# Expert bodies of TensorE in another order, row counts in registers, and narrower constant products

## The chip, the cores and the metric

The kernel runs on one core of a Trainium2 chip. The metric is the device time of one execution in microseconds, median of three runs. TensorE (PE) multiplies matrices and loads its weights beside that (PEld), VectorE (DVE) and ScalarE (ACT) work on vectors, GpSimd (POOL) does odd jobs, SyncE (SP) issues most transfers. Each engine has an instruction stream of its own and waits on counters in shared semaphores.

## The reference

Two layers of a hybrid encoder over 256 tokens of width 1024. Each layer is a token mixer (differential attention, mLSTM, latent attention) and a channel mixer: a dense SwiGLU in layer 0, eight experts in layer 1, of which every token takes its two best.

```python
def swiglu(u, wg, wu, wd):
    return (jax.nn.silu(u @ wg) * (u @ wu)) @ wd

def reference(...):
    for l in range(DEPTH):                      # 2
        shift, scale, gate = ada_modulation(c, w_ada[l, 0], b_ada[l, 0])
        h = rmsnorm(x, g_norm[l, 0]) * (1.0 + scale) + shift
        x = x + gate * rmsnorm(hybrid_mixer(h, positions, l, ...), g_norm[l, 1])
        shift, scale, gate = ada_modulation(c, w_ada[l, 1], b_ada[l, 1])
        h = rmsnorm(x, g_norm[l, 2]) * (1.0 + scale) + shift
        if l % 2 == 0:
            y = swiglu(h, w_gate_d[l // 2], w_up_d[l // 2], w_down_d[l // 2])
        else:
            y = moe_swiglu(h, w_router[l // 2], b_router[l // 2], w_gate_e[l // 2], w_up_e[l // 2], w_down_e[l // 2])
        x = x + gate * rmsnorm(y, g_norm[l, 3])
    return x
```

In `moe_swiglu` the router's two best experts of each token are found, the tokens are sorted by expert, `swiglu` is applied to each expert's rows with its own weights (1024 x 3584 twice, 3584 x 1024 once), and each token's two results are added with their gates.

## The kernel before

Layer 0 and the mixer of layer 1 take the first 680 us. Their weights come through a ring of seven slots. What this case is about is the loop over the eight experts, from about 680 us to the end, and how each engine finds its code in it.

**Rows.** The number of rows of each expert is known only on the chip (tensor `cnt`, filled by the router). It is rounded up to one of six sizes (`NVAR`, 32, 64, 128, 160, 192, 256), and for each size there is a body of code. With these inputs the experts 0 to 7 take the bodies 32, 32, 128, 64, 160, 32, 192 and 64. In the trace a body is known by its line: 32 and 64 rows by L1449 (gate and up) and L1463 (down), in `expert_whole`; 160 and 192 by L1492 and L1507, in `expert_wide`; 128 by L1584 and L1623, in `expert_split`. The last two kinds take part of the weights as pairs of narrower numbers that ScalarE and VectorE make (`parts`), the first kind takes them as they are.

**Stages.** The 3584 columns of an expert are 14 stages. In each PE multiplies the rows (`mixT`, in the code `xe`) by the gate and up weights into the bank `PG`, ScalarE takes Silu, VectorE the product, PE turns it (`turn`, L1435), VectorE copies it out (L2581), and PE multiplies it by the down weights into `Y`. The first stage of the wide bodies uses the banks `TRB` too.

**Weights.** An expert's weights are 42 pieces of 1 MB ("uses"), in 14 slots (`ring` and `arena`). SP issues one transfer for each (`expert_use`, L787) in the order of use, when PE has signalled its last read of the piece that was in the slot 14 uses before. So SP can be up to 14 pieces ahead of PE, and across the border between two experts too.

**Rows of the next expert.** GpSimd copies them into `xe` (L2782 for the first, L2789 in its loop) after the last gate and up product of the expert before, and raises `xe_ready`, on which PE waits ahead of each body.

**The loop.** `experts` (L670) writes the same skeleton of blocks for PE, VectorE and ScalarE: `next` counts `turn` up and ends the loop, `pick` loads this expert's count from `cnt` into the register `rows`, a chain of tests (`tree` and `not_...`, L693 and L695) compares it with the sizes, and the bodies follow, each ending in a branch to `next`, with a hint to the hardware placed at the body's head (L698). The body of 128 rows stands first, right behind the tests, and is reached by falling through all of them; the others stand behind it by size (32, 64, 160, 192, 256) and are reached by a taken branch. The tests for smaller sizes come first (L693), then those for larger ones, from 256 down (L695).

**Constant products.** `busy` (L845) lets PE multiply a constant by the identity into a bank that nobody reads. It stands in `stats` (L861), three products of 256 columns ahead of a wait for VectorE's `diag` (L880), at seven places that run one after the other through the program, and once ahead of `gather` (L1393), four products of 256 columns.

**Reading the instruction rows.** One product of 4-byte floats is carried out in several passes, and each pass is an instruction of its own in the trace: a count of x64 at L1449 is 64 passes.

## Time and profile before

| | |
|---|---|
| median of three runs | 1666.01 us (1665.38, 1666.01, 1673.49) |
| profiled execution | 1666.87 us |
| its span, first to last instruction | 1665.0 us |
| PE busy | 1475.6 us, 89% of the span |
| PEld | 1186.7 us, 71% |
| VectorE | 781.7 us, 47% |
| ScalarE | 589.5 us, 35% |
| GpSimd | 69.4 us, 4% |
| moved by DMA | 488.89 MB, mean 294 GB/s |

PE is busy for 89% of the span. That is a mean over stages with different limits: in the experts of 32 rows PE is idle for part of each stage while the DMA engines are always occupied, in the wider ones it is the other way round. Branches, register and semaphore instructions aren't counted as busy. "Issue" as the reason for idle time means that the engine waited for nothing that the profile can name: no semaphore, no transfer, no engine.

### The profile page before, as it was taken

To read this page: it belongs to the slowest core of one execution; us is meant where nothing else is said; L and a number is where in the kernel's file an instruction comes from. 1 tells how busy PE (TensorE), PEld (TensorE's weight loads), DVE (VectorE), ACT (ScalarE), POOL (GpSimd) and SP (SyncE) were. 2 spreads that over 40 slices of the span, in tenths; PEclk is the share of its full clock that TensorE was granted. 3 is DMA by queue.
4 is the path that set the end of the run, shared out by engine and by line. 5 is a ranking of instruction groups with operands and counts; after the bars stand their busy time and mean duration, and the time that the engine had idled before them with its cause. 6 is when DMAs were issued, how large, how long until landed. Compare 5 with 4: busy or idle time off the path is not lost.

```text
span 1665.0 us, 30777 instructions
## 1 busy us (share of the span) xinstructions
PE 1475.6 (89%) x12430; PEld 1186.7 (71%) x12431; DVE 781.7 (47%) x1097; ACT 589.5 (35%) x793; POOL 69.4 (4%) x67
## 2 busy tenths in 40 slices
PE   5999899999999998765679999999997589999894
PEld 3868778999977886644447875589885468888452
DVE  2574565666546654200019861166761046665112
ACT  2445244444343532100017750055641035554101
POOL 0010100000010111000000000000000000000002
PEclk9999999999999999987779999999999889999997
DMA  9645367745423627899999999997778996666893
GB/s 349 234 154 201 157 250 284 296 177 203 163 96 127 228 77 317 367 425 424 424 425 426 426 421 421 425 425 287 263 250 361 424 424 265 224 226 225 308 426 140
DMA packets 69183, 488.89 MB, mean 294 GB/s; under 512 B 7744, under 2 KB 7776, under 8 KB 11168
## 3 DMA queue, kind: packets, MB, share of 16 engines
q1 hardware_dynamic: 66800, 479.94, 72.3%
q10 hardware_dynamic: 1648, 4.59, 0.8%
q8 instruction: 117, 1.92, 0.5%
q0 software_dynamic: 576, 2.10, 0.4%
q14 instruction: 42, 0.34, 0.1%
HBM read 482.66 MB, written 3.93 MB: 292 GB/s over the span
## 4 chain that ended last, share of the span: by engine, by line
PE 45%; DMA 10%; issue 4%; DVE 2%; SPq 1%; ACT 1%; POOL 0%; ACTq 0%; POOLq 0%; DVEq 0%
PE PG L1449 9%; DMA arena<-in_experts 6%; PE PG L1507 4%; PE PG L1571 4%; PE Y L1534 4%; PE Y L1463 4%; PE TRB L1507 4%; DMA ring<-in_experts 3%; PE TRB L1513 3%; PE PG L1513 3%; PE Y L1623 2%; PE Y L1525 2%; PE TRB L1435 2%; SPq L787 1%; PE PG L1492 1%
## 5 line engine op out<-in xcount | busy, mean ns | idle before, releaser
L2581 DVE COPY arena<-TRB 128x64 f32<-128x64 f32 (+1 forms) x70 | 17.6, 252 | 339.9 <-PE TRB L1435 339.9
L1449 PE MATMUL PG<-ring,mixT 128*32 128x128 f32 (+1 forms) x1920 | 119.8, 352 | 56.9 <-issue 56.7
L1687 ACT ACTIVATE rope<-PG 64x128 f32<-64x128 f32 (+2 forms) x84 | 27.1, 323 | 373.8 <-PE PG L1449 352.1
L1449 PEld LDWEIGHTS PG<-ring,mixT 128*32 128x32 f32 (+1 forms) x1920 | 91.6, 139 | 88.1 <-issue 73.0
L951 PE MATMUL PG<-h_parts,parts 128*128 128x512 f32 x432 | 152.9, 394 | 1.4 <-DVE arena L2459 1.4
L1687 ACT ACTIVATE parts<-ring 128x2048 fp32r<-128x2048 f32 x81 | 151.8, 1901 | 6.1 <-DMA ring<-in_weights 2.8
L1449 PE MATMUL PG<-arena,mixT 128*32 128x128 f32 (+1 forms) x1664 | 99.5, 343 | 47.6 <-issue 47.6
L1449 PEld LDWEIGHTS PG<-arena,mixT 128*32 128x32 f32 (+1 forms) x1664 | 76.7, 135 | 75.4 <-issue 62.2
L953 PE MATMUL PG<-h_parts,parts 128*128 128x256 f32 x432 | 121.8, 282 | 0.0
L2444 DVE TENSOR_TENSOR parts<-ring,parts 128x2048 fp32r<-128x2048 f32 x42 | 95.1, 2290 | 29.2 <-ACT parts L1687 29.2
L2565 DVE TENSOR_TENSOR parts<-arena,parts 128x2048 fp32r<-128x2048 f32 x42 | 95.3, 2288 | 17.0 <-PE Y L1525 14.4
L2565 DVE TENSOR_TENSOR ring_parts<-ring,parts 128x2048 fp32r<-128x2048 f32 x39 | 88.4, 2288 | 25.0 <-PE Y L1525 13.2
L951 PEld LDWEIGHTS PG<-h_parts,parts 128*128 128x128 f32 x432 | 81.2, 188 | 19.8 <-DVE arena L2459 1.6
L953 PEld LDWEIGHTS PG<-h_parts,parts 128*128 128x128 f32 x432 | 81.3, 188 | 0.0
L1687 ACT ACTIVATE parts<-arena 128x2048 fp32r<-128x2048 f32 x42 | 78.9, 1902 | 4.7 <-PE PG L1571 4.1
L918 PE MATMUL Y<-parts 128*128 128x256 f32 x224 | 63.5, 283 | 0.2 <-DVE parts L2468 0.2
L920 PE MATMUL Y<-parts 128*128 128x256 f32 x224 | 63.4, 283 | 0.0
L919 PE MATMUL Y<-parts 128*128 128x256 f32 x224 | 63.4, 283 | 0.0
L2134 DVE TENSOR_TENSOR ring_parts<-ring,ring_parts 128x2048 fp32r<-128x2048 f32 (+1 forms) x24 | 52.8, 2199 | 18.9 <-ACT ring_parts L1687 18.8
L2565 DVE TENSOR_TENSOR parts<-arena,scr_parts 128x2048 fp32r<-128x2048 f32 x21 | 48.1, 2293 | 26.6 <-ACT scr_parts L1687 26.6
L1687 ACT ACTIVATE ring_parts<-ring 128x2048 fp32r<-128x2048 f32 (+1 forms) x24 | 43.8, 1837 | 41.3 <-PE Y L1258 30.2
L1687 ACT ACTIVATE arena<-PG 128x512 f32<-128x512 f32 x29 | 17.3, 597 | 114.5 <-PE PG L953 105.6
(385 smaller groups left out, 2881.4 us busy)
## 6 DMA issues: line engine op xcount, KB each, us to landing
ring<-in_experts SPq DMA_DIRECT2D x168, 1024.0 KB, 16.7
arena<-in_experts SPq DMA_DIRECT2D x168, 1024.0 KB, 17.5
ring<-in_weights SPq DMA_DIRECT2D x116, 1024.0 KB, 6.4
ring<-in_weights SPq DMA_DIRECT2D x4, 512.0 KB, 4.9
ypairs<-hT ACTq DMA_DIRECT2D x3, 512.0 KB, 5.7
tok<-in_x SPq DMA_DIRECT2D x1, 1024.0 KB, 9.2
result<-scr SPq DMA_DIRECT2D x2, 512.0 KB, 2.6
ring<-in_weights SPq DMA_DIRECT2D x2, 432.0 KB, 5.5
```

Source lines behind the costliest of these rows:

```text
L918: mm(out_, w_hi[w][:, c], x[0], start=first, stop=False, skip_group_check=True)
L951: mm(PG[:, m, :].rearrange("p (i t) -> p i t", i=2), w_hi[d % SPLITS][:, c], h_parts[:, :, k, :], start=(k == 0), stop=False, skip_group_c ...
L953: last = mm(PG[:, m, 0:T], w_lo[d % SPLITS][:, c], h_hi[:, k, :], start=False, stop=(k == KD - 1), skip_group_check=True)
L1449: last = mm(bank[i * n:(i + 1) * n, 0:width], xe[:, k, 0:n], w[k // 4][:, k % 4, i * width:(i + 1) * width], start=(k == 0), stop=(k == KD ...
L1463: last = mm(o, actT[:, s % 2, f, 0:n], w[:, f, c:c + width], start=(s == 0 and f == 0), stop=(s == STAGES - 1 and f == 1))
L1507: last = mm(both, hi[:, k, i // 2, i % 2, :], h_parts[:, :, h * KD // 2 + k, 0:n], start=(h == 0 and k == 0), stop=False, skip_group_check ...
L1513: last = mm(bank[:, 0:n], lo[:, k, i // 2, i % 2, :], h_parts[:, 0, h * KD // 2 + k, 0:n], start=False, stop=(h == 1 and k == KD // 2 - 1) ...
L1534: last = mm(o, a[:, s % 2, f, :], w[:, f, c:c + width], start=(opens and s == 0 and f == 0), stop=(closes and s == STAGES - 1 and f == 1))
L1571: last = mm(bank, x[j][:, h * KD // 2 + k, :], w[:, k, :], start=(opens and k == 0), stop=(closes and k == KD // 2 - 1))
L1687: return nc.scalar.activation(out_, in_, func, **kw)
L2444: V.tensor_tensor(w_lo[d % SPLITS], ring[:, slot_of[slot_of_dense(d)], :, :].rearrange("p k c -> p (k c)"), w_hi[d % SPLITS].bitcast(F32), ...
L2565: V.tensor_tensor(w_lo_e[q % SLOTS_E], ring_e[q % SLOTS_E].rearrange("p k c -> p (k c)"), w_hi_e[q % HI].bitcast(F32), ALU.subtract).then_ ...
```

## The change

1. `experts` takes the order of the bodies as a table, `layout`; its first entry is the body behind the tests. PE gets (32, 192, 64, 160, 128, 256). VectorE and ScalarE keep the default, which is the order of before.
2. On each of the three engines the eight counts are loaded ahead of the loop into eight registers (`to_come`). The tests read the first of them, and `next` moves all the others down by one. The block `pick` is gone.
3. `busy` cuts its products: six of 128 columns for three of 256 in `stats`, sixteen of 64 for four of 256 ahead of `gather`.

```diff
--- before.py
+++ after.py
@@ -667,23 +667,26 @@
             u, n = proj_use(l, key)
             return (ring_parts[:, slot_of[i], 0:n].rearrange("p (k c) -> p k c", k=KD) for i in (u + 1, u))
 
-        def experts(eng, name, emit, first_variant=128):
+        def experts(eng, name, emit, layout=(128, 32, 64, 160, 192, 256)):
+
+            first_variant = layout[0]
 
             def label(x):
                 return f"{name}_{x}"
 
             own = [eng.engine]
             turn = eng.alloc_register(label("e"))
-            rows = eng.alloc_register(label("rows"))
+            to_come = [eng.alloc_register(label(f"rows_{i}")) for i in range(NE)]
+            rows = to_come[0]
+            for i in range(NE):
+                eng.reg_load(to_come[i], cnt[0:1, i:i + 1])
             eng.reg_mov(turn, 0)
-            eng.br(label("pick"))
+            eng.br(label("tree"))
             with nc.body(label("next"), valid_engines=own):
                 eng.reg_add(turn, turn, 1)
-                eng.br_lt(turn, NE, on_true=label("pick"), on_false=label("done"))
-            with nc.body(label("pick"), valid_engines=own):
-                e = eng.snap(turn, min_val=0, max_val=NE - 1)
-                eng.reg_load(rows, cnt[0:1, bass.ds(e, 1)])
-                eng.br(label("tree"))
+                for i in range(NE - 1):
+                    eng.reg_mov(to_come[i], to_come[i + 1])
+                eng.br_lt(turn, NE, on_true=label("tree"), on_false=label("done"))
 
             tests = [n for n in NVAR if n < first_variant] + [n for n in reversed(NVAR) if n > first_variant]
             after = [label(f"not_{n}") for n in tests[:-1]] + [label(first_variant)]
@@ -693,7 +696,7 @@
                         eng.br_lt(rows, n + 1, on_true=label(n), on_false=then)
                     else:
                         eng.br_lt(rows, NVAR[NVAR.index(n) - 1] + 1, on_true=then, on_false=label(n))
-            for n in sorted(NVAR, key=lambda n: n != first_variant):
+            for n in layout:
                 with nc.body(label(n), valid_engines=own):
                     back = eng.mark_branch_hint_location()
                     emit(eng.snap(turn, min_val=0, max_val=NE - 1), n)
@@ -874,7 +877,7 @@
                     last = mm(bank[:, b:b + 1], s4[:, b * P:(b + 1) * P], ones[:, 0:1], start=True, stop=True)
                 last.then_inc(tr_full, 1)
                 bank = take_tr((kind, n, "laid"))
-                busy(bank, 3)
+                busy(bank, 3, 2)
                 pe.wait_ge(diag_ready, q + 1)
                 for b in range(TB):
                     last = mm(bank[:, b * P:(b + 1) * P], ones[:, :], diag[:, b, :], start=True, stop=True)
@@ -1387,7 +1390,7 @@
                skip_group_check=True).then_inc(tr_full, 1)
 
 
-            busy(xg_banks[0], 4)
+            busy(xg_banks[0], 4, 4)
 
             def gather(k, b, part, columns, first=False):
                 return mm(xg_banks[k][:, columns], part[:, b, k * P:(k + 1) * P], sel[:, b, columns],
@@ -1663,7 +1666,7 @@
                 pe.wait_ge(xe_ready, e + 1)
                 (expert_whole if n < P else expert_split if n % P == 0 else expert_wide)(e, n)
 
-            experts(pe, "pe", expert)
+            experts(pe, "pe", expert, layout=(32, 192, 64, 160, 128, 256))
 
             for b in range(TB):
                 for k in range(KD):
```

**PE at the loop's head.** The rows below are the instructions in the order of the program. Before, from the last products ahead of the loop (L1393) through counting (L681), the end test (L682), the load of the count (L685) and the tests to the body of 128 rows (from L1421):

```order
L1393 MATMUL TRB<-parts,h_parts 128x512 x8
L679 UNCONDITIONAL_BRANCH
L681 REGISTER_ALU
L682 COMPARE_AND_BRANCH
L684 ISA
L685 TENSOR_LOAD cnt
L686 UNCONDITIONAL_BRANCH
L693 COMPARE_AND_BRANCH x2
L695 COMPARE_AND_BRANCH x3
L698 BRANCH_PREFETCH_HINT
L699 ISA
```

After, the same place:

```order
L1396 MATMUL TRB<-parts,h_parts 128x512 x8
L682 TENSOR_LOAD cnt x8
L684 UNCONDITIONAL_BRANCH
L686 ISA
L689 COMPARE_AND_BRANCH
L698 COMPARE_AND_BRANCH x5
L701 BRANCH_PREFETCH_HINT
L702 ISA
L1424 ISA
L1452 MATMUL PG<-ring,mixT 32x128 x64
```

The loads of the counts stand ahead of the loop, five tests of one kind lead to the body behind them, and that body begins with products of 32 rows.

**PE where one body ends and the next stands.** Before, the end of the body of 128 rows (L1623) and the head of that of 32 rows (L1449):

```order
L1623 MATMUL Y<-parts 128x512 x4
L1623 MATMUL Y<-parts,arow_parts 128x512 x4
L1623 MATMUL Y<-parts 128x512 x4
L700 UNCONDITIONAL_BRANCH
L698 BRANCH_PREFETCH_HINT
L699 ISA
L1421 ISA
L1449 MATMUL PG<-ring,mixT 32x128 x64
```

After, the end of the body of 32 rows (L1466) and the head of that of 192 rows (L1495):

```order
L1461 REGISTER_ALU
L1466 MATMUL Y<-arena 32x256 x8
L703 UNCONDITIONAL_BRANCH
L701 BRANCH_PREFETCH_HINT
L702 ISA
L1424 ISA
L1495 MATMUL PG<-mixT,ring 128x192 x8
```

What stood between the bodies of 128 and 64 rows (32) now stands ahead of all, followed by 192; likewise 64 follows 192, 160 follows 64, and 128, which was first, follows 160.

## Rows read from the trace of the kernel before

**Rows 1.** Busy time by stage: us, busy of each engine, PEclk, DMA share, GB/s

```profile
690.00:1078.00 388.00, 317.80 (x3254) 227.02 (x3253) 126.90 (x157) 101.62 (x117) 8.11 (x4) 0.91 1.01 424
...
1142.00:1254.00 112.00, 110.49 (x833) 98.07 (x833) 76.82 (x63) 61.10 (x62) 1.90 (x1) 1.00 0.71 259
```

**Rows 2.** PE in time: start, length, line, operation, passes, [idle before <-what ended it]

```profile
664.03 1.06 PE L849 MATMUL TRB<-con 128*128 128x128 f32 x8
...
665.56 1.97 PE L849 MATMUL PG<-con 128*128 128x256 f32 x8
...
669.22 0.95 PE L1393 MATMUL PG<-parts,h_parts 128*128 128x256 f32 x6 [1.69 <-DVE parts L2535]
...
681.01 4.28 PE L1449 MATMUL PG<-ring,mixT 128*32 128x128 f32 x76 [4.04 <-issue]
...
765.89 3.22 PE L1449 MATMUL PG<-ring,mixT 128*32 128x128 f32 x56 [7.38 <-issue]
...
771.33 3.70 PE L1449 MATMUL PG<-ring,mixT 128*32 128x128 f32 x72 [2.22 <-issue]
...
866.98 7.13 PE L1584 MATMUL PG<-ring,mixT 128*128 128x512 f32 x16 [0.74 <-issue]
...
881.30 1.21 PE L1623 MATMUL Y<-parts 128*128 128x512 f32 x4 [1.35 <-DVE arow_parts L2573]
...
990.91 3.24 PE L1449 MATMUL PG<-ring,mixT 128*64 128x256 f32 x28
...
995.02 4.11 PE L1449 MATMUL PG<-ring,mixT 128*64 128x256 f32 x36 [0.86 <-issue]
...
1067.83 3.67 PE L1449 MATMUL PG<-arena,mixT 128*64 128x256 f32 x32 [1.12 <-issue]
...
1082.92 1.62 PE L1492 MATMUL TRB<-mixT,ring 128*128 128x160 f32 x10 [1.50 <-issue]
...
1259.16 3.22 PE L1449 MATMUL PG<-ring,mixT 128*32 128x128 f32 x56 [4.59 <-issue]
...
1344.30 4.65 PE L1492 MATMUL PG<-mixT,ring 128*128 128x192 f32 x16 [6.91 <-issue]
...
1551.99 9.17 PE L1449 MATMUL PG<-ring,mixT 128*64 128x256 f32 x64 [5.66 <-issue]
```

**Rows 3.** Branches of PE's sequencer by switch: ns min/median/max, first and last start in us

```profile
L693 PEldq COMPARE_BRANCH  x1: 6561/6561/6561, 673.9 to 673.9; - x1
...
L693 PEldq COMPARE_BRANCH  x1: 6488/6488/6488, 758.9 to 758.9; - x1
...
L695 PEldq COMPARE_BRANCH  x3: 65/65/68, 866.3 to 866.6; - x3
...
L693 PEldq COMPARE_BRANCH  x2: 67/210/352, 988.9 to 989.1; - x2
...
L695 PEldq COMPARE_BRANCH  x3: 65/68/447, 1076.6 to 1076.9; - x3
...
L693 PEldq COMPARE_BRANCH  x1: 4007/4007/4007, 1254.6 to 1254.6; - x1
...
L695 PEldq COMPARE_BRANCH  x2: 68/3179/6290, 1337.5 to 1337.6; - x2
...
L693 PEldq COMPARE_BRANCH  x2: 67/2520/4972, 1546.4 to 1546.5; - x2
```

**Rows 4.** The page, DMA queues: packets, MB, share of 16 engines

```profile
q8 instruction: 117, 1.92, 0.5%
```

**Rows 5.** GpSimd in time: the first expert's rows, two copies

```profile
677.10 2.02 POOL L2782 COPY mixT<-arena 128x1536 f32<-128x1536 f32 x2 [21.36 <-PE TRB L1393]
```

**Rows 6.** Line 685, the count's load: ns min/median/max, first and last start

```profile
L685 PEldq TENSOR_LOAD <-cnt x8: 302/306/495, 673.4 to 1546.0; - x8
```

**Rows 7.** ScalarE's sequencer at the head of its last body, window 1550 to 1557

```profile
L698 ACTq BRANCH_PREFETCH_HINT  x1: 55/55/55, 1555.5 to 1555.5; - x1
```

**Rows 8.** Line 880: idle time before it by releaser, us and times

```profile
  DVE diag L2086: 4.2, 8
```

## The prediction

> **What bounds the kernel now.** I read the page first, then the busy time by stage, then PE's instructions in order of time around each change of expert, then the branches of PE's sequencer, which the page's busy times leave out. From 690 to 1078 us the DMA engines are occupied all the time (share 1.01); from 1142 to 1254 they are at 0.71 while PE is at 110.49 of 112 us [rows 1]. So experts 0, 1 and 5 (32 rows) run at the pace of their weights, experts 2, 4, 6 and 7 (128, 160, 192, 64 rows) at PE's, and expert 3 (64 rows) starts at PE's pace and is caught by its weights at its end: two stages there begin only when their weights have landed, after 1.03 us (at 1060.54, not shown) and 1.12 us [rows 2]. From this follows what a gap of PE between two experts costs: nothing between experts 0 and 1, and all of it ahead of a body at PE's pace. Ahead of a body that waits for weights it costs the time by which the first freed slot comes later.
>
> Such gaps there are: 4.04, 7.38, 0.74, 4.59, 6.91 and 5.66 us ahead of bodies, and 2.22, 0.86, 1.50 us inside them, all "issue" [rows 2]. Under them lie branches. PE's branches take 0.06 to 0.09 us when they fall through, but 6.56, 6.49, 4.01, 6.29 and 4.97 us when they jump to the body of experts 0, 1, 5, 6 and 7; the jumps to the bodies of experts 3 and 4 took 0.35 and 0.45 us, and expert 2 was reached by falling through [rows 3]. PE's code arrives by DMA: 117 packets of 16 KB [rows 4], which is 256 instructions of 64 bytes. The rule that I take from these rows: a jump is cheap when its target stands in the packet with which the body that ran before ended (64 after 32, 160 after 64), or in the packet of the loop's tests, which every body brings back at its end; a body that has not been read lately costs a fetch. Where the packet ends soon after the target, a second wait follows: 56 products after the start of the 32-row body PE stands still for 2.22 us [rows 2].
>
> **The new order, body by body.** The experts' rows are 32, 32, 128, 64, 160, 32, 192, 64. In front of the tests now stands 32 instead of 128; 192 follows 32, 64 follows 192, 160 follows 64. Counting the built program's instructions from the places of the second waits, the packets end 96 instructions after the start of the 32-row body, 39 after 192, 143 after 64, 128 after 160, and 8 after 128.
>
> *Expert 0.* The 6.56 us branch becomes a fall-through, but PE can't begin before GpSimd's copy of the rows is done at 679.1 [rows 5]. PE begins at 679.2 instead of 681.01, the first slot is freed as much earlier, and all transfers behind it shift: -2.0. Eight register loads ahead of it, 0.3 us each [rows 6], begin while PE still works on its queue (673.4) and end before 679.
>
> *Expert 1.* 7.38 us saved under saturated DMA: 0.
>
> *Expert 2* was the fall-through and is now far off. Nearest rows: the jump ahead of expert 1, made under the same full DMA: 7.38 idle, then from 765.89 to 771.33 until the second packet is there. With only 8 instructions in the first packet nearly nothing runs in between, so both count: 7.38 + 5.44 - 0.74 as it is now = 12.1. After such a stall PE runs at 1.2 GHz for a while: 64 products took 9.17 us at 1551.99 where 32 took 3.67 at 1067.83 [rows 2], so 1.8 us more. Against it, a wait of 1.35 us for VectorE in the first stage goes, since the helpers get ahead. Together +12.5; at least 0 (body found at hand), 7.1 with one fetch, at most 15.
>
> *Expert 3.* The 0.35 us jump becomes a fetch of 4.0 to 6.5, taken as 5.5. The sequencer jumps at 989.1, 1.8 us before the array has finished at 990.9 [rows 2, 3]: 5.5 - 1.8 + 0.4 to the first product = 4.1 idle, + 1.8 for the clock, - 0.86 (143 instructions last through the next fetch): +5.0; from 0 to 8. PE, now some 15 us late, no longer meets the two waits for weights at this expert's end: -2.15. Transfers are issued by freed slots, but they are queued far ahead and move less than PE.
>
> *Expert 4.* The stall of 1.50 goes, but VectorE's own first steps bind right behind: -0.4, from 0 to -1.5.
>
> *Expert 5.* 4.59 idle becomes about 1.2 (branches and tests), and PE stays at 2.4 GHz. The first freed slot comes 5 us earlier; the transfers close up to what was queued: -4.4, from -3 to -5.
>
> *Expert 6.* 6.91 idle becomes 0.9, but after 39 instructions (17 products) a wait of about 2.9 follows (5.6 us for the fetch, as from 765.5 to 771.3, less 2.8 of work). With the clock's 1.8 back, and half of it lost again in that wait: -6.0 + 2.9 - 1.8 + 0.2 = -4.7; from -3 to -7.
>
> *Expert 7.* 5.66 idle becomes about 1.2, and the clock stays up: PE alone would gain 6.3. But ScalarE, whose code has its old order, reaches its 64-row body only at 1555.5 [rows 7]; table load, Silu and VectorE's product end near 1558, and PE's turning of them, now at 1561.1, can't be earlier: -3.0, less 0.5 for an idle PE before it: -2.5, from -1 to -6.
>
> **Tests and registers.** A load of 0.3 us [rows 6] a turn goes for eight moves of registers, and the 32-row body now takes five tests of 0.07 each instead of one. Within 0.3 us a turn either way, for the most part in the shadow of PE's queue: 0.
>
> **Narrower constant products.** Eight passes of 256 columns took 1.97 us, eight of 128 took 1.06 [rows 2]: 12 for 6 cost 0.1 us at each of seven places, where PE then waits for VectorE's diagonal, 4.2 us in eight waits [rows 8], 0.5 each. The other place has 1.69 us of waiting behind it. Cost 0; without that cover 0.8.
>
> **Sum:** -2.0 + 12.5 + 5.0 - 2.15 - 0.4 - 4.4 - 4.7 - 2.5 = +1.35 us on the profiled execution's 1666.87: 1668.2. The median of the three runs is 0.86 lower, so 1667.4.
>
> The Trainium skill ("Runtime: NRT & Kernel Launch", Instruction fetch mechanics) gives PE's instruction memory as a FIFO of 128 KiB in blocks of 256 instructions. The trace agrees: the start of the 64-row body outlived the 128-row body, but not a 32-row body and more. The same section says that there are only two lines, and a taken branch outside this window must fetch. By that rule the jump ahead of expert 3 would have cost a fetch before, too, and the change would lose nothing there; the sum would be about -3.7. The 0.35 us of that jump speaks against it.
>
> **Rivals.** (1) *One fetch ahead of expert 2*, should the packet behind the target be asked for with it: 12.5 becomes 7.1, 1662.0. Against it: three starts of the 32-row body after a fetch, two of them with a second wait. (2) *No new fetches*, should a hint at the loop's head or a larger memory hold the far bodies: the sum is -2.0 - 0.4 - 4.4 - 4.7 - 2.5 = -14.0, 1652.0. For it: two cheap jumps far back in time; against it: their targets had been read, as ends of the body before, and those of 128 and 64 would not have been. (3) *Slower: the neighbours are not kept.* A body's last packet is also where the loop's packet is called back; should the start of 192 or 64 be gone by the time of the jump, experts 6 and 7 save nothing (+7.2), and expert 2 may reach its upper price (+2.5): 1677. It decides from the point at which the target's packet has to be read again. Rows of 0.35 and 0.45 us speak against it. (4) *Nothing changes*, since all bodies wait for weights: 1666.
>
> **Chances.** Forecast 0.55 (1661 to 1673), rival 1 0.12, rival 2 0.15, rival 3 0.12, rival 4 0.06. About 0.5%, 8.3 us, is what a measurement of this kernel can tell from none: faster 0.22 (rival 2 and the low edge of rival 1), same 0.63, slower 0.15. The range goes from 1654 to 1677.
>
> **What the profile after would show.** Ahead of the first product of 128 rows an idle time near 12 us in two pieces; ahead of expert 3's first product 4; no branch over 1 us ahead of experts 0, 1, 4, 5, 6, 7; a short stall after some 17 products of 192 columns; ScalarE's table load of expert 7 still near 1556 by the old clock of events, with PE waiting for it. A single short gap ahead of expert 2 means rival 1, none rival 2; a branch of 4 us or more ahead of expert 6 or 7 means rival 3. I am wrong in the sum if delays in experts 2 and 3 turn out to be covered by transfers, or if the granted clock after the stalls is other than before.

## The result: slower by 0.47%, just outside the range

The changed kernel takes 1677.19 us (median of 18 runs, 1670.29 to 1686.4), the kernel before 1670.77 us in the same 18 rounds (1664.25 to 1680.0). The ratio on record is 1.0047, 95% interval 1.0033 to 1.0062 (the two medians by themselves give 1.0038): slower by 0.47%, 7.8 us on 1666.01. The forecast was 1667.4, a rise of 1.4 us, with a range to 1677.0. The time is 0.2 us above that range; 7.8 us on 1666.01 would be 1673.8 and inside it, since the kernel before was slower in these rounds too. Either way the rise is more than five times the one forecast. The profiled execution took 1676.06 us.

The page of the changed kernel, span, busy times and the two queues that carry code:

```profile
span 1674.3 us, 30896 instructions
PE 1484.9 (89%) x12496; PEld 1194.3 (71%) x12496; DVE 781.8 (47%) x1096; ACT 589.4 (35%) x793; POOL 69.4 (4%) x67
...
q8 instruction: 113, 1.85, 0.5%
...
q14 instruction: 42, 0.34, 0.1%
```

PE is busy for 9.3 us more, though the products are the same but for their widths. About 1.5 us of it is the narrower products (an estimate from the pages of runs 1 and 5 below, 1480.4 and 1478.9 us); for the rest, passes behind a stall run at 1.2 GHz and take longer. q8 carries PE's code, 16 KB a packet. q14 carries packets of 8 KB; several of them move when VectorE and ScalarE change bodies (six from 1548 to 1560 us in the kernel before), which is why it is read here as the queue of their code. The page of before had this second queue too; the prediction hadn't used it.

PE in order of time around the changes of expert (columns as in [rows 2]):

```profile
680.04 1.29 PE L1452 MATMUL PG<-ring,mixT 128*32 128x128 f32 x20 [2.39 <-POOL mixT L2785]
...
870.29 2.07 PE L1587 MATMUL PG<-ring,mixT 128*128 128x512 f32 x2 [7.68 <-issue]
875.38 6.93 PE L1587 MATMUL PG<-ring,mixT 128*128 128x512 f32 x9 [3.02 <-issue]
...
1004.29 3.98 PE L1452 MATMUL PG<-ring,mixT 128*64 128x256 f32 x20 [4.20 <-issue]
...
1265.91 4.19 PE L1452 MATMUL PG<-ring,mixT 128*32 128x128 f32 x128 [0.76 <-issue]
1276.83 0.76 PE L1438 MATMUL TRB<-con,rope 64*128 64x128 f32 x2 [6.74 <-DVE rope L2562]
...
1348.88 2.86 PE L1495 MATMUL PG<-mixT,ring 128*128 128x192 f32 x16 [0.45 <-issue]
1354.95 3.28 PE L1495 MATMUL TRB<-mixT,ring 128*128 128x192 f32 x12 [3.21 <-issue]
...
1555.33 7.13 PE L1452 MATMUL PG<-ring,mixT 128*64 128x256 f32 x64 [1.17 <-issue]
1567.28 0.97 PE L1438 MATMUL TRB<-con,rope 64*128 64x128 f32 x3 [4.83 <-DVE rope L2562]
```

Almost every row is where the prediction put it: expert 0 begins when GpSimd's copy is done; 7.68 and 3.02 us in two pieces ahead of expert 2, with two passes between them; 4.20 ahead of expert 3; none ahead of 5, 6 and 7; 3.21 after 16 products of 192 columns. What it had not put there are the two rows that end with "<-DVE rope": in experts 5 and 7 PE starts at once, runs through two units of gate and up products and then stands still for 6.74 and 4.83 us.

From such rows comes the account by expert. An expert ends with its last product into `Y`; the table shows how much later each kernel got there than the kernel before, from one expert's end to the next, in the profiled executions. "Ahead" is the work up to the loop, which varies from one execution to another with no reason in the loop (up to 9.5 us), "loop" is from there to the last instruction, without "ahead".

| us against before | ahead | e0, e1 | e2 | e3 | e4 | e5 | e6 | e7 | tail | loop | ratio of the times |
|---|---|---|---|---|---|---|---|---|---|---|---|
| forecast | | -2.0 | +12.5 | +2.85 | -0.4 | -4.4 | -4.7 | -2.5 | 0 | +1.35 | 1.001 |
| changed kernel | +0.7 | -4.3 | +12.8 | +2.2 | -0.7 | +0.5 | -3.2 | 0.0 | +1.4 | +8.6 | 1.0047 |
| run 1, old order | +0.4 | +1.0 | +4.9 | -3.2 | -0.7 | -1.3 | +5.3 | -0.4 | -0.3 | +5.3 | 1.0036 |
| run 2, order alone | +5.9 | -2.9 | +9.0 | +5.7 | +3.9 | -0.1 | +0.7 | +2.9 | +0.6 | +19.8 | 1.0088 |
| run 3, order on all | +2.0 | -4.3 | +13.1 | +2.4 | -0.4 | +0.8 | -3.3 | -6.2 | +0.8 | +2.8 | 1.0012 |
| run 4, 128 last | +0.2 | -3.5 | +6.6 | +2.8 | +0.7 | +0.4 | -2.7 | +0.8 | +1.4 | +6.5 | 1.0039 |
| run 5, shift alone | +2.3 | -2.8 | +5.4 | -2.6 | -0.3 | +0.2 | +4.1 | -0.3 | -0.3 | +3.3 | 1.0022 |
| run 6, 64 first, all | +1.0 | +3.8 | +0.4 | +0.1 | -1.0 | -2.2 | +1.4 | -6.8 | +0.4 | -3.9 | 0.9960 |
| run 7, 192 first, all | +3.4 | +1.0 | +1.8 | +3.9 | -0.5 | -1.8 | -3.0 | -1.4 | +1.5 | +1.5 | 0.9987 |
| run 8, 192 first, PE | +0.3 | +0.5 | +2.4 | +3.5 | -0.7 | +1.9 | -8.2 | -2.5 | +1.2 | -2.0 | 0.9982 |
| run 9, shift undone | -0.6 | +3.3 | -0.1 | 0.0 | +0.2 | +0.6 | +1.5 | -1.6 | +0.4 | +4.2 | 1.0020 |
| run 10, both mended | +8.4 | -2.2 | +7.8 | +1.4 | -0.4 | -1.0 | -2.1 | -6.5 | +0.6 | -2.3 | 0.9981 |
| run 11, 32, 128 first | +9.5 | -2.5 | +1.5 | +0.3 | +4.4 | -2.5 | +1.3 | +1.0 | -0.1 | +3.3 | 0.9988 |
| run 12, hint | +0.5 | +0.6 | +1.2 | +0.1 | +0.6 | -1.5 | -0.2 | -6.7 | -0.2 | -6.1 | 0.9959 |
| run 13, helpers alone | -3.4 | -0.2 | +0.4 | -0.5 | +0.1 | 0.0 | 0.0 | +0.2 | 0.0 | 0.0 | 1.0008 |
| run 14, no registers | +6.4 | -2.4 | +0.7 | +0.8 | +0.8 | -2.8 | +1.8 | -6.5 | +0.2 | -7.4 | 0.9963 |

One execution is not a median. Run 13 shows how little may move where PE's code stays as it was; experts 0 and 1 show how much, -2.8 us in run 5 and -0.2 in run 13, with PE's loads and order as before in both. A column of one run is taken here as good to about 2 us, that of experts 0 and 1 to 3 or 4.

### The profile page after: what moved, and what is told of

It is laid out like the page before. It is cut to its first block, busy times and chain, and to the rows that moved or that the text cites. A ratio compares the mean times of both kernels' runs of the same rounds, so it can differ in the third digit from the quotient of the medians.

```text
span 1674.3 us, 30896 instructions
## 1 busy us (share of the span) xinstructions
PE 1484.9 (89%) x12496; PEld 1194.3 (71%) x12496; DVE 781.8 (47%) x1096; ACT 589.4 (35%) x793; POOL 69.4 (4%) x67
## 3 DMA queue, kind: packets, MB, share of 16 engines
q10 hardware_dynamic: 1648, 4.59, 0.8%
## 4 chain that ended last, share of the span: by engine, by line
PE 45%; DMA 8%; issue 5%; DVE 2%; ACT 1%; SPq 1%; POOL 0%; ACTq 0%; DVEq 0%; POOLq 0%
PE PG L1452 9%; DMA arena<-in_experts 5%; PE Y L1466 4%; PE PG L1510 4%; PE Y L1537 4%; PE TRB L1510 4%; PE PG L1574 4%; DMA ring<-in_experts 3%; PE TRB L1516 3%; PE PG L1516 3%; PE Y L1626 2%; PE Y L1528 2%; PE TRB L1438 2%; SPq L790 1%; PE Y L1261 1%
## 5 line engine op out<-in xcount | busy, mean ns | idle before, releaser
L954 PEld LDWEIGHTS PG<-h_parts,parts 128*128 128x128 f32 x432 | 81.2, 188 | 19.8 <-DVE arena L2462 1.6
```

The lines of the kernel that those rows point to most:

```text
L954: mm(PG[:, m, :].rearrange("p (i t) -> p i t", i=2), w_hi[d % SPLITS][:, c], h_parts[:, :, k, :], start=(k == 0), stop=False, skip_group_c ...
```

## Experiments on the changed kernel's loss

The theory after the first look: the order costs what was forecast at expert 2, and the gains at experts 5 and 7 are hidden, since VectorE and ScalarE must fetch their own bodies there. The rivals: registers or products, and weights that come late.

**Run 1: registers and products with the old order.**

```diff
-            experts(pe, "pe", expert, layout=(32, 192, 64, 160, 128, 256))
+            experts(pe, "pe", expert)
```

> The changed kernel with the old order of bodies on TensorE: registers and narrower constant products alone. Theory (instruction packets): expert 2 is again reached by falling through (idle under 1 us), experts 5, 6 and 7 again have idle times of 4 to 7 us ahead of their first product. Only the places of the bodies in their packets move: the 192-row body now has 47 instructions left in its first packet instead of 183, so a second wait of 2 to 3 us follows within the first 25 products of expert 6; the waits of 0.86 and 1.50 us in experts 3 and 4 go. Sum +0.5 to +1 us, ratio to the kernel before 1.000 to 1.001. Rival (the register loads and moves, or the narrower products, cost the time): ratio 1.003 or more, with the loss ahead of the loop or spread over all eight switches.

Measured: ratio 1.0036 (1.0019 to 1.0053), which the theory as written excluded. The loss isn't spread, though: it sits behind the 32-row bodies, in a place that the prediction hadn't counted. The branch from the end of PE's bodies back to the loop's head, first over all eight, then those behind experts 1 and 5:

```profile
L703 PEldq COMPARE_BRANCH  x8: 201/372/5479, 760.2 to 1640.7; - x8
...
L703 PEldq COMPARE_BRANCH  x1: 4126/4126/4126, 866.8 to 866.8; - x1
...
L703 PEldq COMPARE_BRANCH  x1: 5479/5479/5479, 1337.2 to 1337.2; - x1
```

In the kernel before the same branch (L700) took 0.42 us at most. The loop's packet has to be read again too. Behind expert 5 the traces show when: in the kernel before, one packet of PE's code moves between 1326 and 1336.1 us (at 1333.3), ahead of the branch back; in run 1 none moves between 1329.5 and 1337.2, where the branch is met, and the next one comes at 1340.2. The reading that fits both is that the packet is asked for when PE enters the body's last packet. Registers and products put 136 instructions ahead of the bodies (132 of them the products, four for each product more), and with that the 32-row body ends some 75 instructions into its last packet, not 194: too few to last through a fetch. Idle ahead of expert 6 became 11.89 us, two fetches in a row:

```profile
1350.38 1.97 PE L1495 MATMUL PG<-mixT,ring 128*128 128x192 f32 x5 [11.89 <-issue]
```

The second wait that was expected within the first 25 products of expert 6 did not come: the 64 passes of 192 columns that follow run without idle time, the first 16 of them in 4.97 us instead of the 2.86 at full clock.

**Run 2: the order alone, on the kernel before.**

```diff
-        def experts(eng, name, emit, first_variant=128):
+        def experts(eng, name, emit, layout=(128, 32, 64, 160, 192, 256)):
+            first_variant = layout[0]
-            for n in sorted(NVAR, key=lambda n: n != first_variant):
+            for n in layout:
-            experts(pe, "pe", expert)
+            experts(pe, "pe", expert, layout=(32, 192, 64, 160, 128, 256))
```

> The kernel before with nothing but the new order of TensorE's bodies. Theory: the loss comes with the order, but its size depends on where each body starts in its packet. Here the 128-row body has 144 instructions left instead of 8, so expert 2 has one wait of 7 to 8 us and no second one of 3 us: its cost falls from 12.8 us to about 7. The 160-row body now has 8 left: a second wait of 2 to 5 us a few products into expert 4. The 64-row body has 23 left: 1 to 5 us more in expert 3, hidden at expert 7. Experts 5 and 7: TensorE starts 4 us earlier and waits for VectorE and ScalarE, no gain. Sum about +5 to +9 us, ratio 1.003 to 1.005. Rival (registers or products are the cause): ratio 1.000 or below.

Measured: 1.0088 (1.0061 to 1.0114), twice what was expected. Right: one wait ahead of expert 2 (8.47 us) and none behind it; 3.85 us two passes into the 160-row body, of which 8 instructions stand in its first packet:

```profile
1095.90 0.54 PE L1494 MATMUL PG<-mixT,ring 128*128 128x160 f32 x2
1100.29 2.92 PE L1494 MATMUL PG<-mixT,ring 128*128 128x160 f32 x14 [3.85 <-issue]
```

Wrong: again the ends of bodies. The 32-row body ends 82 instructions into its last packet here, and the way back takes up to 5.85 us, so that expert 6 begins after 6.80 us of idle time although its code stands next to expert 5's. So the products aren't harmless: by the count of instructions they are what put the changed kernel's bodies in better places than the order alone would (its 32-row body ends 217 instructions into a packet, and no way back there takes over 0.93 us).

**Run 5: nothing but a shift, on the kernel before.** A block of products that is never executed, between the code ahead of the loop and the loop:

```diff
-            eng.br(label("pick"))
+            if name == "pe":
+                eng.br_lt(turn, NE, on_true=label("pick"), on_false=label("pad"))
+                with nc.body(label("pad"), valid_engines=own):
+                    for _ in range(34):
+                        nc.tensor.matmul(tr[0][:, 0:8], ident, con[:, C_IOTA:C_IOTA + 8], start=True, stop=True)
+                    eng.br(label("next"))
+            else:
+                eng.br(label("pick"))
```

> The kernel before, with a block of TensorE instructions that is never executed between the code ahead of the loop and the loop: nothing is done otherwise, but all bodies stand 137 instructions later, as in the first experiment (registers and products with the old order). Theory (only the place of the code in its packets of 256 instructions cost time there): the 32-row body ends 76 instructions into its last packet instead of 194, too short to hide the fetch of the loop's packet, so TensorE's branch back to the loop takes 4 to 5.5 us after experts 0, 1 and 5; the 192-row body has 46 instructions left in its first packet. Idle time ahead of expert 2 above 4 us instead of 0.74, ahead of expert 6 near 12 instead of 6.91; ratio 1.003 to 1.004. Rival (the registers or the narrower products cost it): the idle times stay as in the kernel before, ratio 1.000.

Measured: 1.0022 (1.0003 to 1.0041), and run 1's pattern in the places where it was expected: +5.4 and +4.1 us at experts 2 and 6, with 4.83 and 10.96 us idle.

```profile
L707 PEldq COMPARE_BRANCH  x1: 3886/3886/3886, 864.9 to 864.9; - x1
...
L707 PEldq COMPARE_BRANCH  x1: 4399/4399/4399, 1338.2 to 1338.2; - x1
```

```profile
1350.40 1.96 PE L1499 MATMUL PG<-mixT,ring 128*128 128x192 f32 x5 [10.96 <-issue]
```

So the place of the code costs time by itself, with the same instructions executed but for one branch.

**Run 9: registers and products, old order, shifted on by 121 to a full packet.** The diff is run 1's, with the block above (30 products) ahead of `tree`.

> The changed kernel with the old order of bodies and with a block of TensorE instructions that is never executed ahead of the loop, so that every body stands 257 instructions behind its old place: at the same place in its packet as in the kernel before. Registers and narrower products are the only things left of the change. Theory (both cost nothing, the place of the code cost what the first experiment lost): TensorE's branch back to the loop is short again (under 0.5 us) after the 32-row bodies, idle ahead of expert 2 under 1 us and ahead of expert 6 about 7 instead of 11.9; ratio 0.999 to 1.001. Rival (loads, moves or products cost it): 1.003 and up, as in the first experiment.

Measured: 1.0020 (1.0003 to 1.0038). The waits behind the 32-row bodies are gone (the way back takes 0.41 us at most, idle is 0.45 ahead of expert 2 and 7.19 ahead of expert 6), as the theory has it. But the ratio isn't 1, and its 3.3 us lie in experts 0 and 1. There the rival has a point. PE's sequencer met the branch to expert 0's body at 673.9 [rows 3]; here, behind eight loads, at 675.8, and its fetch took 7.48 us:

```profile
L703 PEldq COMPARE_BRANCH  x1: 7484/7484/7484, 675.8 to 675.8; - x1
```

```profile
683.84 3.43 PE L1459 MATMUL PG<-ring,mixT 128*32 128x128 f32 x60 [7.46 <-issue]
```

**Run 4: the 128-row body in another place of its packet.**

```diff
-            experts(pe, "pe", expert, layout=(32, 192, 64, 160, 128, 256))
+            experts(pe, "pe", expert, layout=(32, 192, 64, 160, 256, 128))
```

> The changed kernel with the bodies of 128 and 256 rows exchanged on TensorE (32, 192, 64, 160, 256, 128). No expert uses the 256-row body, so only the place of the 128-row body changes: 87 of its instructions stand in its first packet instead of 8. Theory: the jump still costs about 7 us ahead of expert 2, but the second wait of 3 us behind its first products is gone, and the later ones of that stage with it: 4 to 6 us less than the changed kernel, ratio to the kernel before 1.001 to 1.003. Rival (the cost is the distance, or the clock after the stall, not the packet): as the changed kernel, 1.004 to 1.006.

Measured: 1.0039 (1.0014 to 1.0063). In the trace expert 2 costs +6.6 instead of +12.8, 6.2 us less, and one row shows why:

```profile
869.85 8.88 PE L1587 MATMUL PG<-ring,mixT 128*128 128x512 f32 x16 [6.88 <-issue]
```

All sixteen passes run in one piece behind a single fetch. The loop as a whole is 2.1 us below the changed kernel's; the ratio's interval holds both what was expected and no difference. The mechanism at expert 2 is shown, what it is worth at the end is not settled by this run.

## Experiments on experts 5 and 7

**Run 3: the new order on VectorE and ScalarE too.**

```diff
-        def experts(eng, name, emit, layout=(128, 32, 64, 160, 192, 256)):
+        def experts(eng, name, emit, layout=(32, 192, 64, 160, 128, 256)):
```

> The changed kernel with the same new order of bodies on VectorE and ScalarE too. Theory (at experts 5 and 7 their own fetches of code hide TensorE's gain): their branches to the bodies of experts 5 and 7 fall from 4 to 6 us to under 0.5; the idle times of TensorE of 6.74 us (expert 5) and 4.83 us (expert 7) in the first stage shrink to under 2; expert 5 gains about 4 us, expert 7 4 to 5. The cost at expert 2 (12.8) stays. Against the kernel before 0 us, from -2 to +3: ratio 0.999 to 1.002; about 8 us faster than the changed kernel. Rival (the weights, not the code, are late there): the idle times of TensorE stay above 4 us and end with a weight transfer, ratio 1.004 to 1.006 as for the changed kernel.

Measured: 1.0012 (0.9994 to 1.0031), 0.35% below the changed kernel's 1.0047. Expert 7 gains 6.2 us more than in the changed kernel, what the prediction had for PE alone (6.3); the stall is gone:

```profile
1557.65 7.13 PE L1452 MATMUL PG<-ring,mixT 128*64 128x256 f32 x64 [1.12 <-issue]
1564.71 0.71 PE L1438 MATMUL TRB<-con,rope 64*128 64x128 f32 x4
```

ScalarE reaches its body's head 4.3 us behind PE there (1561.5 and 1557.2); in the changed kernel it was 9.9 us (1564.8 and 1554.9). Expert 5 gains nothing, against what was expected: ScalarE is late again (1274.5, PE 1267.7), this time with a way back that is slow, 2.8 us, as PE's were in run 1, and PE waits 4.54 us.

**Run 13: the helpers alone.** On the kernel before, with the order as a table (run 2's diff):

```diff
-        def experts(eng, name, emit, first_variant=128):
+        def experts(eng, name, emit, layout=(64, 160, 32, 128, 192, 256)):
+            first_variant = layout[0]
-            experts(pe, "pe", expert)
+            experts(pe, "pe", expert, layout=(128, 32, 64, 160, 192, 256))
```

> The kernel before with the order 64, 160, 32, 128, 192, 256 on VectorE and ScalarE, and TensorE, its counts and its products as they were. Theory (at experts 5 and 7 two fetches run beside each other, TensorE's and its helpers', and only both together are worth something): the helpers' branches ahead of expert 7 fall from 4 to 6 us to under 0.5, but TensorE still starts 4.6 and 5.7 us late; it then gains 1 to 2 us at most in the first stage of each, and its later helpers at expert 6 (192 rows) fetch beside TensorE's own 6.9 us. Against the kernel before -3 to 0 us, ratio 0.998 to 1.000. Rival (the helpers alone were the bound there): 9 us faster, 0.995.

Measured: 1.0008 (0.9993 to 1.0023), and at most 0.5 us in any expert. The heads of the three engines' bodies at expert 7, and PE:

```profile
L700 DVEq BRANCH_PREFETCH_HINT  x1: 39/39/39, 1544.4 to 1544.4; - x1
L700 PEldq BRANCH_PREFETCH_HINT  x1: 41/41/41, 1548.1 to 1548.1; - x1
L700 ACTq BRANCH_PREFETCH_HINT  x1: 51/51/51, 1548.3 to 1548.3; - x1
```

```profile
1548.54 9.17 PE L1451 MATMUL PG<-ring,mixT 128*64 128x256 f32 x64 [5.81 <-issue]
1557.64 0.71 PE L1437 MATMUL TRB<-con,rope 64*128 64x128 f32 x4
```

Counted from the end of expert 6, VectorE is ready 5.5 us and ScalarE 3.6 us earlier than in the kernel before. PE is not, and the time is the same. The changed kernel is the other half of the pair: there PE's fetch is gone and the helpers' is not, and experts 5 and 7 gain nothing either (+0.5, 0.0). At expert 7, where run 3 has both away, 6.2 us are won. So two fetches run beside each other there, and taking either away alone is worth nothing.

**Runs 7 and 8: 192 first, on all three engines and on TensorE alone.** Both have ten products of 128 columns ahead of the gathering, to set the packets.

```diff
-            busy(xg_banks[0], 4, 4)
+            busy(xg_banks[0], 5, 2)
-            experts(pe, "pe", expert, layout=(32, 192, 64, 160, 128, 256))
+            experts(pe, "pe", expert, layout=(192, 64, 160, 32, 128, 256))
```

Run 7 gives `experts` this order as its default too.

> The changed kernel with the order 192, 64, 160, 32, 128, 256 on all three engines, and ten products of 128 columns instead of sixteen of 64 ahead of the gathering, which sets the packets. By the packet theory only expert 3 (64 after 128) fetches: 4 to 6 us idle ahead of it, of which its late weights give 2 back. Expert 6 is reached in the loop's packet: its 6.9 us go. Sum against the kernel before: expert 2 0, expert 3 +2.5, expert 4 -1, expert 5 -4, expert 6 -5.5, expert 7 -5.5: -13, ratio 0.991 to 0.994. Rival (as before): 0.997 to 1.001.

> As the run before, but with the new order on TensorE alone; VectorE and ScalarE keep the old one. Theory: their own fetches ahead of experts 5 and 7 (4 to 6 us) hide TensorE's gain there: it starts within 1.2 us and then waits 4 to 7 us for VectorE in the first stage. Sum 8 to 9 us less gain than with the order on all: ratio 0.996 to 0.999. Rival (TensorE's own fetch is what counts): within 2 us of the run with the order on all.

Measured: 0.9987 (0.9969 to 1.0006) and 0.9982 (0.9965 to 1.0000): no difference between them, where 8 to 9 us were expected. At expert 5 the theory holds: TensorE alone gains nothing (+1.9, with 4.98 us of waiting for VectorE), with all three it gains 1.8. At expert 7 it fails: TensorE alone gains 2.5 us and with all three 1.4, since PE itself is late in both (3.81 and 3.85 us idle) and never waits for VectorE. Run 8:

```profile
1549.73 8.50 PE L1452 MATMUL PG<-ring,mixT 128*64 128x256 f32 x64 [3.81 <-issue]
1558.16 0.71 PE L1438 MATMUL TRB<-con,rope 64*128 64x128 f32 x4
```

That comes from another end of a body, that of 192 rows, 32 instructions into its packet: the way back took 3.3 and 3.4 us. And the theory was blind for what the helpers pay at expert 6. With their new order ScalarE's way back from expert 5 takes 4.5 us (1347.9 to 1352.4), and it reaches its 192-row body 7.5 us behind PE, with the old order 3.3 us (PE and ScalarE, run 7 first):

```profile
L701 PEldq BRANCH_PREFETCH_HINT  x1: 36/36/36, 1345.2 to 1345.2; - x1
...
L701 ACTq BRANCH_PREFETCH_HINT  x1: 60/60/60, 1352.7 to 1352.7; - x1
```

```profile
L701 PEldq BRANCH_PREFETCH_HINT  x1: 40/40/40, 1345.3 to 1345.3; - x1
...
L701 ACTq BRANCH_PREFETCH_HINT  x1: 50/50/50, 1348.6 to 1348.6; - x1
```

and PE then waits 4.36 us for VectorE in run 7, and gains 3.0 us at expert 6 where run 8 gains 8.2.

**Run 10: the two repairs together.** Run 3's diff and run 4's.

> The changed kernel with the two repairs together: VectorE and ScalarE in the new order too, and TensorE's 128-row body behind that of 256 rows, where 87 of its instructions stand in its first packet. Theory: the two losses are separate (one sits in expert 2, the other in experts 5 and 7), so their repairs add up: 6 us in expert 2, 4 to 5 in experts 5 and 7 together. Against the kernel before 0 to -4: ratio 0.997 to 1.000. Rival (what is won in expert 2 is lost to late weights): ratio as with the order on all alone, 1.001.

Measured: 0.9981 (0.9963 to 0.9998), as expected: +7.8 us at expert 2 for the changed kernel's +12.8, -6.5 at expert 7 for 0.0. It is 0.66% below the changed kernel, and both parts of that have their expert.

## Experiments towards a faster version

**Run 6: 64, 160, 32, 128, 192, 256 on all three engines**, with counts in registers and the products of before. With this order PE needs a fetch only ahead of expert 0 and for two changes of body, 32 to 32 and 32 to 192.

> Counts in registers, products as before, and the order 64, 160, 32, 128, 192, 256 on all three engines. By the packet theory every change of expert but 32 to 192 and 32 to 32 finds its code at hand, and the 32-row body ends 220 instructions into its last packet. Against the kernel before: expert 2 0 to +1, expert 3 -1, expert 4 -1, expert 5 -4, expert 6 0 (its fetch of 6.9 us stays), expert 7 -5: 9 to 11 us faster, ratio 0.993 to 0.995. Rival (gains of TensorE are covered by weights that come late): 0.998 to 1.001 with idle times of TensorE that end with a transfer.

Measured: 0.9960 (0.9943 to 0.9978), 1663.04 us: faster than both kernels, by 0.4 instead of 0.6%. Expert 7 gains 6.8 us. Experts 0 and 1 lose 3.8, for which nothing was written: expert 0's body is now far off and its branch is met behind the loads (677.3, 7.5 us). Expert 5 gains 2.2 instead of 4, with a second wait, 92 instructions behind its head:

```profile
1259.51 1.47 PE L1452 MATMUL PG<-ring,mixT 128*32 128x128 f32 x43 [0.59 <-issue]
1263.33 4.27 PE L1452 MATMUL PG<-ring,mixT 128*32 128x128 f32 x85 [2.35 <-issue]
```

**Run 12: run 6 with a hint** for the 32-row body ahead of the gathering.

```diff
+            early = pe.mark_branch_hint_location()
             busy(xg_banks[0], 4)
...
-                        eng.br_lt(rows, n + 1, on_true=label(n), on_false=then)
+                        back = eng.br_lt(rows, n + 1, on_true=label(n), on_false=then)
+                        if early is not None and n == 32:
+                            back.branch_hint(early)
```

> The kernel of the sixth run (64, 160, 32, 128, 192, 256 on all engines) with one prefetch hint more, ahead of the gathering (100 instructions and 12 us before the loop), for the 32-row body. Theory: the fetch of 7.5 us ahead of expert 0, which starts the whole chain of weights 4 us late, is over before the branch; TensorE starts expert 0 near 680 instead of 685.4, and experts 0 and 1 end 4 to 8 us earlier: ratio 0.991 to 0.994. Rival (the hinted packet takes the place of the next one of the straight code, or is gone again when the branch comes): the same wait inside the gathering or at the branch, ratio 0.996 as without it.

Measured: 0.9959 (0.9942 to 0.9975), as run 6: the time is as the rival has it. The hint is executed at 665.5, and the branch still takes 5.1 us (7.5 in run 6, and 5.7 to 7.5 in the five runs with the loads and no hint).

```profile
L1395 PEldq BRANCH_PREFETCH_HINT  x1: 41/41/41, 665.5 to 665.5; - x1
...
L696 PEldq COMPARE_BRANCH  x1: 5143/5143/5143, 677.0 to 677.0; - x1
```

The trace shows that the hint fetched nothing: no packet of PE's code moves between 662 and 679.5 us, and the first one comes at 679.8, behind the branch at 677.0. So the rival's reason, a packet that comes and is pushed out again, is wrong. Why the hint asks for nothing is not shown. The waits of runs 1 and 2 speak for a fetch of the loop's packet that starts when the last packet is entered, not when the hint is executed; perhaps a hint must stand ahead of such an entry, and this one stood behind it.

**Run 11: 32, 128, 64, 160, 192, 256 on all engines.** Twelve products of 64 columns ahead of the gathering.

> Counts in registers, the order 32, 128, 64, 160, 192, 256 on all three engines, twelve products of 64 columns ahead of the gathering, which sets the packets. Expert 0 starts with code at hand, and 32 to 32, 32 to 128, 128 to 64, 64 to 160, 160 to 32 need no fetch; 32 to 192 and 192 to 64 do, as before. Theory: experts 0 and 1 -3.5 us, 3 and 4 -1 each, 5 -4, 6 and 7 0: -9, ratio 0.993 to 0.996. Rival (weights are late instead): 0.998 to 1.001.

Measured: 0.9988 (0.9971 to 1.0005); expected was 0.993 to 0.996. Experts 0 and 1 (-2.5) and 5 (-2.5) gain, but a branch back of 5.96 us ahead of expert 4 costs 4.4, although the 64-row body ends 74 instructions into its last packet, and its products are three times as long as those of 32 rows. The count of instructions alone doesn't forecast that.

**Run 14: run 6's order, one load a turn as before.** Run 13's diff, with (64, 160, 32, 128, 192, 256) on TensorE too.

> The kernel before with the order 64, 160, 32, 128, 192, 256 on all three engines and nothing else: one load of a count a turn instead of eight ahead of the loop. The bodies stand within 4 instructions of the sixth run's. Theory: with a fetch ahead of expert 0, the eight loads put its start off by 2.6 us (the branch is met at 673.9 us before, at 675.8 to 676.9 with them), and all transfers up to expert 1's end with it. So without them TensorE starts expert 0 about 2.5 us earlier: ratio 0.993 to 0.996, 2 to 3 us below the sixth run. Rival (the loads lie in the shadow, and moves in registers are worth their place later): as the sixth run or above, 0.996 to 0.998.

Measured: 0.9963 (0.9946 to 0.9980), run 6: 0.9960. In the trace experts 0 and 1 take 6.2 us less than in run 6, and PE is idle for 3.44 us ahead of expert 0, not 7.47. Over all runs the idle time there is 3.4 to 4.2 us without the loads (before, runs 5, 13, 14) and 5.1 to 7.5 with them where a fetch follows (runs 1, 6, 7, 8, 9, 12). That the loads put the start off is shown; that it is worth 2 to 3 us at the end is not, since the ratios of 6 and 14 don't differ.

## Why the prediction was wrong, point by point

The fetches of PE's code were forecast rightly, place by place. What failed is what PE's earlier starts at experts 5, 7 and 6 were said to be worth: ScalarE's arrival was left out at expert 5 and taken as a fixed time at expert 7, and the clock was said to stay up or come back.

**Experts 0 and 1**: -2.0 forecast, -4.3 measured, -2.2 to -4.3 in the six kernels with 32 rows first. PE starts when the copy is done, as forecast. Only the size is off.

**Expert 2**: +12.5 forecast, +12.8 measured, by the two fetches that were forecast; run 4 takes one of them away, and 6.2 us go. Rivals 1 and 2 fall.

**Expert 3**: +5.0 - 2.15 forecast, +2.2 measured (4.20 us idle; 4.1 was worked out). **Expert 4**: -0.4, measured -0.7.

**Expert 6**: -4.7 forecast, -3.2 measured. Idle went from 6.91 to 0.45 and 3.21 came behind 16 passes (2.9 was worked out), together -3.25. The term that failed is the clock, -1.8 + 0.2: behind the new stall PE is at the lower level again. The sum also had a slip: half of 1.8 is 0.9, not 0.2, and with 0.9 it would have been -4.0. Busy time of the changed kernel by stretch (columns as in [rows 1]):

```profile
1348.00:1352.00 4.00, 3.29 (x24) 2.73 (x17) 1.80 (x3) 0.75 (x2) 0.00 (x0) 1.00 1.03 424
1352.00:1355.00 3.00, 0.05 (x1) 0.05 (x1) 0.00 (x0) 1.93 (x3) 0.00 (x0) 1.00 0.99 404
1355.00:1358.00 3.00, 3.00 (x12) 3.00 (x12) 1.50 (x1) 2.15 (x2) 0.00 (x0) 0.62 1.00 421
```

The granted share is 1.00 before and 0.62 behind the 3 us of idle time, a stretch with both levels in it; in the kernel before it was 0.60 from 1344 to 1349, behind 6.91 us. The stall moved, and the clock's loss moved with it.

**Expert 5**: -4.4 forecast, +0.5 measured: the largest miss. The step that failed is "4.59 idle becomes about 1.2": it does (0.76), and it was never the bound: in the kernel before, too, PE's turning of the first unit waited for VectorE, if only 0.46 us:

```profile
1265.70 0.46 PE L1435 MATMUL TRB<-con,rope 64*128 64x128 f32 x2 [0.46 <-DVE rope L2559]
```

Each body's first stage needs three engines, and I followed only PE's code. ScalarE stood at its body's head at 1261.9 before and 1274.5 after, 12.6 us later, where PE had ended expert 4 only 10.6 us later. PE's turning of the first unit comes 11.1 us later, whatever PE gains ahead of it. And where code is at hand on all engines, expert 5 gives 1.5 to 2.8 us (runs 6, 7, 11, 12, 14), not 4.4. That its weights are the next bound is argued, not shown by a run: in the kernel before the DMA share is 1.01 from 1266 to 1340.

**Expert 7**: -2.5 forecast, 0.0 measured. Here I had ScalarE in the sum, but as a fixed time. It isn't one: it comes from the end of expert 6 plus a fetch, and both moved. The branch was met at 1551.7 before, with the head at 1555.5 [rows 7], 3.9 us; after it was:

```profile
L696 ACTq COMPARE_BRANCH  x2: 34/42/50, 1558.5 to 1558.5; - x2
...
L701 ACTq BRANCH_PREFETCH_HINT  x1: 51/51/51, 1564.8 to 1564.8; - x1
```

6.3 us. What goes with the longer fetch is PE's own early start. The DMA engines while ScalarE waited, before and then after:

```profile
1552.00:1556.00 4.00, 4.00 (x20) 2.53 (x22) 0.00 (x0) 0.00 (x0) 0.00 (x0) 0.50 0.33 97
```

```profile
1560.00:1565.00 5.00, 2.45 (x24) 1.61 (x20) 0.00 (x0) 0.00 (x0) 0.00 (x0) 1.00 0.99 403
```

Before, PE and its helpers fetched together while hardly a weight moved (share 0.33). Now PE frees slots at once, SP issues transfers, the share is 0.99, and the helpers' code travels among the weights. That the share is the reason for the longer fetch is the reading of these rows; no run varied it alone. For ScalarE eight traces with the helpers in the old order agree with it, though in most of the first group PE fetched beside it too: at experts 5 and 7 of the kernel before, runs 1, 5 and 9, and at expert 7 of run 2, its fetch took 2.2 to 4.6 us with the share over the fetch at 0.41 to 0.60; in the changed kernel, runs 4 and 8, and at expert 5 of run 2, it took 4.6 to 6.3 us with 0.74 to 1.01. VectorE's fetch ahead of expert 7 hardly differs, 5.7 us before and 6.3 after, with 0.88 and 0.89.

This step alone doesn't make 0.0. Counted from the end of expert 6, ScalarE's head is 1.5 us later than before, and PE's turning of the first unit is still 1.6 us earlier (13.1 us instead of 14.8). The second step that failed is "the clock stays up": behind the 4.83 us of waiting it is down again,

```profile
1567.00:1571.00 4.00, 3.72 (x18) 2.47 (x20) 0.95 (x3) 0.00 (x0) 0.00 (x0) 0.57 0.90 373
```

the turning (its four passes) takes 1.19 us instead of 0.71 and the next 32 passes 4.82 instead of 3.67, and with that the 1.6 us are gone.

The Trainium skill ("Runtime: NRT & Kernel Launch", Instruction fetch mechanics) has crossing from one block of code to the next as mostly hidden; here it cost 2.22 to 3.85 us in the rows above, where the packet ended behind the first 2 to 56 passes of a body, and nothing in runs 1 and 5 at expert 6, where the clock was down and the passes took longer.

**Registers and products at 0.** In the changed kernel this holds, since GpSimd's copy covers the loads (2.39 idle "<-POOL"). It is an answer about a cover: with a fetch behind them the loads show (run 9). The products are nearly free as work, but they are 132 instructions, and run 5 shows what a shift of 137 costs the old order: 0.22% (0.03 to 0.41). I had counted the bodies' heads in the built program, and not their ends.

**Sum.** The misses are experts 5 (+4.9), 7 (+2.5) and 6 (+1.5), experts 0 and 1 (-2.3), 3 and 4 (-1.0), 2 (+0.3) and the tail (+1.4): together the 7.3 us by which the loop's +8.6 is above +1.35. The tail's 1.4 us lie in the store of the last results, from which GpSimd gathers: its first gather starts 5.0 us behind the issue of `ypairs<-hT`, not 3.4. Nothing in the change bears on that, and the tail was between -0.3 and +1.5 in the other runs. The rival with the slower result (neighbours not kept) was wrong: all of them were kept.

**What stays open.** Why ScalarE's branch back was slow in run 3, and why a body that ends 74 instructions into its packet had to wait (run 11) where one with 18 did not (128 rows in run 5). The rule of heads and ends finds the places that are at risk, not each wait.

## What to carry to other kernels

Where a loop jumps between bodies of code, its cost is a fetch on every engine that takes part, side by side: work out the first stage for all of them, and mend all or none. A gain of one engine is worth what the next late one leaves, and an engine that starts earlier also starts its transfers earlier, it seems into the way of the others' code. And an edit ahead of such a loop shifts every body: look at where heads and ends of bodies fall before a fraction of a per cent is put down to the edit itself.

## What the runs showed of the hardware that was not expected

- A shift of 137 never executed instructions made the same work slower by 0.22% (run 5, 0.03 to 0.41); the order alone, in bad places, by 0.88% (run 2).
- The branch back to a loop's head, which carries a hint, took up to 5.48 us (run 1), 5.85 (run 2) and 5.96 (run 11); in the kernel before it took 0.2 to 0.42.
- Code for engines other than PE came in packets of 8 KB. ScalarE's fetch took 2.2 to 4.6 us with the DMA share at 0.41 to 0.60, and 4.6 to 6.3 with 0.74 to 1.01 (experts 5 and 7 in eight traces).
- A prefetch hint executed once, 11.5 us ahead of its branch, moved no packet of code (run 12: none from 662 to 679.5 us, the branch at 677.0 took 5.1 us).
- Behind 3 us of idle time the granted clock was 0.62 of full speed for the next 3 us; behind 6.91 us in the kernel before it was 0.60 for 5 us.
